# A two-layer diffusion trunk on one core: Silu of an expert's first tile ahead of a weight split, later waits for the last operand tiles, and filler products on TensorE

## What is computed

```python
def swiglu(h, w1, w3, w2):                       # layer 0: 1024 -> 2816 -> 1024
    return (jax.nn.silu(h @ w1) * (h @ w3)) @ w2

def moe_swiglu(h, router_w, router_b, w1, w3, w2):   # layer 1: 8 experts, 1024 -> 1024 -> 1024
    ...
    top_v, top_i = lax.top_k(logits, TOP_K)
    gates = jax.nn.softmax(top_v, axis=-1)
    ...
    hid = jax.nn.silu(jnp.einsum('nd,edf->enf', t, w1)) * jnp.einsum('nd,edf->enf', t, w3)
    hid = hid * dense_g.T.astype(hid.dtype)[:, :, None]
    return jnp.einsum('enf,efd->nd', hid, w2).reshape(b, s, d)
```

## Time and profile before

| | us |
|---|---|
| median of 3 runs | 1968.56 (1968.44 to 1970.23) |
| the profiled execution | 1969.62 |
| its span, first to last instruction | 1967.8 |
| PE busy | 1744.9 |
| DVE busy | 1162.0 |
| ACT busy | 649.0 |
| POOL busy | 259.3 |

### The profile page before, as it was taken

The page is one execution under the profiler, slowest core; times in us unless marked ns, Lnnn a source line. Parts: engine busy times, 40 slices in busy tenths (PEclk is TensorE's granted clock), DMA queues, the critical chain, the costliest instruction groups (busy, mean ns, idle before and its releaser), DMA issues.

```text
span 1967.8 us, 29448 instructions
## 1 busy us (share of the span) xinstructions
PE 1744.9 (89%) x11709; PEld 1589.2 (81%) x11709; DVE 1162.0 (59%) x1460; ACT 649.0 (33%) x769; POOL 259.3 (13%) x265
## 2 busy tenths in 40 slices
PE   0599689879999999997888989699999999999996
PEld 0599345779999999997864659588998998998996
DVE  7947567885465666658534663545555555655563
ACT  2221145233311211123322441543444344444431
POOL 3000102320000000003010123130110110110100
PEclk9999689889999999998995989889999999999998
DMA  8244000223344443433110001455555565565552
GB/s 345 70 155 143 20 0 1 86 86 129 101 137 147 149 150 128 160 128 98 65 44 3 0 0 65 179 180 177 203 184 175 200 198 168 208 193 174 208 187 60
DMA packets 45320, 251.13 MB, mean 128 GB/s; under 512 B 5516, under 2 KB 6172, under 8 KB 23888
## 3 DMA queue, kind: packets, MB, share of 16 engines
q1 hardware_dynamic: 28176, 192.17, 26.9%
q0 software_dynamic: 16512, 57.93, 10.1%
q10 hardware_dynamic: 576, 0.26, 0.0%
HBM read 236.68 MB, written 13.72 MB: 127 GB/s over the span
## 4 chain that ended last, share of the span: by engine, by line
PE 79%; DVE 9%; issue 6%; ACT 4%; DMA 1%; POOL 1%; ACTq 0%; DVEq 0%; SPq 0%; POOLq 0%
PE pp L610 55%; PE popr L610 5%; PE pm L610 5%; PE popr L773 4%; DVE popr L1225 3%; PE pp L876 2%; PE pp L727 1%; PE pm L708 1%; PE popr L713 1%; PE pm L753 1%; PE popr L770 1%; PE pm L756 1%; DVE tmpB L1252 1%; PE pm L700 1%; DVE h_lo L1270 1%
## 5 line engine op out<-in xcount | busy, mean ns | idle before, releaser
L1568 DVE TENSOR_TENSOR w_lo<-raw,w_hi 128x2048 fp32r<-128x2048 f32 x108 | 247.4, 2291 | 191.9 <-ACT w_hi L1136 191.9
L610 PE MATMUL pp<-g_hi,w_hi 128*128 128x192 f32 x1152 | 322.4, 280 | 21.3 <-ACT tmpA L1151 19.2
L610 PE MATMUL pp<-g_lo,w_hi 128*128 128x192 f32 x1152 | 321.4, 279 | 0.0
L610 PE MATMUL pp<-g_hi,w_lo 128*128 128x192 f32 x1152 | 321.3, 279 | 0.0
L610 PE MATMUL pp<-h_hi,w_hi 128*128 128x320 f32 x1152 | 267.2, 314 | 49.6 <-DVE h_lo L1270 44.8
L610 PE MATMUL pp<-h_lo,w_hi 128*128 128x320 f32 x1152 | 265.6, 312 | 0.0
L610 PE MATMUL pp<-h_hi,w_lo 128*128 128x320 f32 x1152 | 265.1, 312 | 0.0
L610 PEld LDWEIGHTS pp<-g_hi,w_hi 128*128 128x128 f32 x1152 | 227.4, 197 | 22.8 <-issue 22.8
L610 PEld LDWEIGHTS pp<-h_hi,w_hi 128*128 128x128 f32 x1152 | 195.3, 191 | 52.8 <-issue 51.6
L610 PEld LDWEIGHTS pp<-g_lo,w_hi 128*128 128x128 f32 x1152 | 227.6, 198 | 0.0
L610 PEld LDWEIGHTS pp<-g_hi,w_lo 128*128 128x128 f32 x1152 | 227.4, 197 | 0.0
(11 more groups left out here) (237 smaller groups left out, 3064.6 us busy)
## 6 DMA issues: line engine op xcount, KB each, us to landing
raw<-in_ws SPq DMA_DIRECT2D x164, 1024.0 KB, 4.8
modraw<-in_wmod POOLq DMA_DIRECT2D x80, 512.0 KB, 3.6
mod_first<-in_wmod SPq DMA_DIRECT2D x4, 2048.0 KB, 19.7
out_y<-six SPq DMA_DIRECT2D x7, 512.0 KB, 3.4
xT<-in_xT SPq DMA_DIRECT2D x1, 2560.0 KB, 20.3
token_rows<-tok SPq DMA_DIRECT2D x5, 512.0 KB, 2.6
mixer<-in_mixer SPq DMA_DIRECT2D x1, 1497.0 KB, 25.2
scond<-in_cond SPq DMA_DIRECT2D x1, 1024.0 KB, 5.1
```

The source lines that it names most:

```text
L610: ins = mm(out[:, at_bank(lo, hi)], x, y[:, lo:hi], start=f, stop=end)
L1568: V.tensor_tensor(w_lo[b][:], raw[b][:], w_hi[b][:].bitcast(F32), ALU.subtract).then_inc(w_lo_done, 1)
```

## The change

It has four parts. In each item, ACT now takes Silu of the first tile ahead of the split of slab 2, with no wait of its own for that split. PE starts the output part of an item when two `e_lo` tiles are still to come, and waits for these ahead of the matmuls that read them (`f` = 6 and 7). The same is done in the dense SwiGLU, by a new argument `late` of `slab`. And PE multiplies the two constants 40 times between `find_first` and the wait for the first item's rows, and 6 times behind each of its two gathers (`keep_pace`); nothing reads these products.

```diff
@@ slab
+            def slab(s, t, b_hi, b_lo, n=TOK, kk=KT, it=0, sstep=0, tstep=0, ready=None, order=range(KT), late=None):
...
                     for kt in range(kk):
+                        if late is not None and c == 0 and kt >= kk - 2:
+                            pe.wait_ge(prod_lo, late - kk + kt + 1)
@@ ffn
-                    pe.wait_ge(prod_lo, p)
+                    pe.wait_ge(prod_lo, p - 2)
                     with pe.Fori(0, 2) as i:
                         for c in range(2):
-                            slab(s + c, t + 2 * c, fh_hi, fh_lo, kk=hidden, it=i, sstep=2, tstep=4)
+                            slab(s + c, t + 2 * c, fh_hi, fh_lo, kk=hidden, it=i, sstep=2, tstep=4, late=None if c else p)
@@ experts, PE
+                def keep_pace(n):
+
+                    for _ in range(n):
+                        mm(prow[:, 0:P], ones, ident, start=True, stop=True)
...
                         if n == 0:
-                            pe.wait_ge(prod_lo, j * 8 + (P_MOE + 8))
+                            pe.wait_ge(prod_lo, j * 8 + (P_MOE + 6))
...
                             for f in range(8):
+                                if n == 0 and sl == 0 and f >= 6:
+                                    pe.wait_ge(prod_lo, j * 8 + (P_MOE + f + 1))
...
                 find_first()
+                keep_pace(40)
                 pe.wait_ge(rows_in, 32)
                 for x in range(2):
                     gather(0, x, T_MOE + x)
+                    keep_pace(6)
@@ experts, ACT
                     for i in range(4):
                         t = T_W13 + 4 * i
-                        act.wait_ge(tile_done, j * ITEM_TILES + (t if i else t + 1))
-                        hi_item(j, 2 * i + 2)
+                        if i:
+                            act.wait_ge(tile_done, j * ITEM_TILES + t)
+                            hi_item(j, 2 * i + 2)
                         for m in range(2):
                             act.wait_ge(tile_done, j * ITEM_TILES + (t + m + 1))
                             A(tA(m, CAP), pp[(t + m) % 2][:, 0:CAP], ACT.Silu).then_inc(tile_free[(t + m) % 2], 1)
+                            if i == 0 and m == 0:
+                                hi_item(j, 2)
```

More of the change, by code:

```diff
@@ L611, in three @@
                 return ins
-            def slab(s, t, b_hi, b_lo, n=TOK, kk=KT, it=0, sstep=0, tstep=0, ready=None, order=range(KT)):
+            def slab(s, t, b_hi, b_lo, n=TOK, kk=KT, it=0, sstep=0, tstep=0, ready=None, order=range(KT), late=None):
                 if ready is not None:
```

## The result

The changed kernel takes 1917.86 us (median of 4 runs, 1911.96 to 1919.77); the kernel before, run beside it, takes 1968.71 (4 runs, 1968.44 to 1970.23). The ratio is 0.9736, with a 95% interval from 0.9716 to 0.9756. The forecast was 1915.9. The profiled execution took 1919.68 with a span of 1917.9, so between the two profiled executions the span is 49.9 us shorter.

A forecast was written before the change was run, and what follows sets the result against it. PE, busy for 89% of the span, was taken as the bound, so gaps and low clock must go. 28.3 + 13.3 + 9.5 + 4.2 - 2.6 = 52.7 us off 1968.56 gave 1915.9 us; own range 1911 to 1920, with rival 1910 to 1924.

The forecast's parts named there:

- Part 1: Items 1 to 7: Silu of tile 0 ahead of slab 2's split ends PE's `tmpA` stall, gaining 28.3 us.
- 4.27: 384 matmuls of an item, 42.75 us against 47.02: 2.57 of stall, 1.63 of clock, 0.07 of rounding.
- three conditions: Items 1 to 7: one table load, ahead of the tile's wait; slab 2's later split harmless; queues behind cost PE nothing.
- second rival: ACT in items: table load stays behind the tile's wait, 4.3 us less gain, 1920.2 us; chance 0.09.
- Part 2: Late waits: `e_lo` gaps of nine items 13.3 us, three dense SwiGLU stalls 9.5 us, dense SwiGLU clock 4.2 us.
- first rival: The clock's falls are not owed to PE's stalls and stay: gain 38.7, 1929.9 us; chance 0.08.
- Part 3: `keep_pace` around item 0's gathers: buys nothing, as the DMA chain sets tile 4; a clock fall may lose 2.6 us.
- third rival: Slab weight loads become the bound, PE waits beyond 9.1 us per load; 1975 us at 9.72 us; chance 0.02.
- the fourth: Nothing changes, as slab loads at 9.65 us hold an item at its 75 us: 1968.6 us; chance 0.03.

The follow-up runs named there:

- the experiment with the second wait: Changed kernel with a second, long-met wait of ACT ahead of Silu of tile 0 in each item: 1923.06 us, ratio 0.9765.
- the last experiments: Changed kernel with SP loading slabs 3 and 4 of item 0 ahead of its slot-table wait: 1912.79 us with the constant products, 1912.76 without.
- the one with the filled stall: Kernel before, with 8 constant products put into the stall ahead of tile 2 of every item, Silu still late: 1963.84 us, ratio 0.9972.

## Why the prediction was right, step by step

**Part 1**, 28.3 us: right to the hundredth per item. 70.68 us from item to item with this part alone is 74.95 - 4.27, and item 8 was the right model for the changed item. Its three conditions held. The load went ahead of the wait (1351.90, tile at 1357.7), and the experiment with the second wait showed what it is worth, 4.6 us, beside the 4.3 that stood in the second rival. PE never waits for `tmpB` in items 1 to 7. And nothing queued behind `keep_to` or the slab loads made PE wait in items 1 to 7.

**Part 2**, 13.3 + 9.5 + 4.2: the gaps closed and no matmul waited. The dense SwiGLU gave 14.5 for 13.7, in which the stalls are 9.5 and the clock 5.0 where I had 4.2. The prediction added the items' 1.48 to the 4.27, and in the presence of part 1 that is right: 70.68 - 69.12 = 1.56 per item. As a price of the edit alone it is wrong, and so was my expectation of that experiment: alone it gives 5.5 us. The parts measured one by one give 25.8 + 5.5 + 12.9 - 0.5 = 43.7 us, the whole 50.9. The 7 us between them are, as far as the rows tell, the clock's: with the late waits alone the remaining stall takes 7.9 us more of lower clock, and with that stall filled or closed it takes none.

**The clock.** That the falls are owed to the stalls (the first rival denied it, at 1929.9 us) is shown by filling them: seven items of seven at 37.77 us. Why one item of the kernel before had the stall and no fall is not shown. The Trainium skill ("TensorE: Matmul & The Clock Gate", Why this matters for your kernels) allows a longer gap than these 2.4 us; the runs here don't agree with that allowance, as stalls of 2.40 us cost up to 3.25 us behind them, and closed or filled they cost none.

**Part 3**, nothing: shown twice, 1972.01 for 1971.51 alone and 1919.66 for 1917.86 when taken out. The reason given was SP's queue behind the table of slots, and the last experiments show it: with those two loads moved, the wait is gone. The idle time ahead of tile 4 was forecast at 7.5 us and was about 4.7. Tile 0 began 8.8 us behind the rows (1270.00 to 1278.76), not 7.0, as the clock was low in the first six products between the gathers; and slab 3's split came 19.6 us behind the rows, not 20.5. The rows themselves arrived 1.2 us later behind the routing than without the products, 16.4 us for 15.3 (from 1253.58 and 1263.49), which the prediction had at nothing: tile 0 takes some 2.5 us less and starts 2.2 us later. The price of a product, 0.24 us or more by rows of 32 columns, was near the 0.23 of 128 columns, with no reason given for the width not to count. The clock's loss behind the idle time was 2.1 us for a forecast of 2.6, and the e_lo gap of item 0 was gained.

**The term that was missing** is the 4.5 us of lower clock in the norm, the input projection and `qk_norm` of layer 1, whose code no edit touches. My own range had 2 us for clock falls in attention that shift by chance, but as a gain; as a loss it had only "here and there". Against it stand small errors the other way: 0.8 in the dense SwiGLU, 0.6 in item 0, 0.6 in items 1 to 8. By the two spans the gain is 52.7 + 0.8 + 0.6 + 0.6 - 4.5 - 0.3 = 49.9. The forecast of each edited stretch held within 0.8 us; that the total came within 2 us of the median, 1917.86, is in part luck, as 2.0 us of small errors stood against the missing 4.5.

The third rival (the weights) and the fourth (nothing) had no part in it: PE waits for no `w_lo` in the items at 69.12 us, nor in the version with item 0 shortened.

**Left open:** why the norm's clock falls in five executions and not in two of kernels that have the same code up to there, and why `qk_norm` is slow in just the seven executions whose program holds constant products further on. Open too is what makes the scatter between runs. The changed kernel had 8 us between its slowest and fastest run, where the kernel before had 2 in the same comparison, but in the three later ones, of more runs, the kernel before had 8 to 11, so nothing shows the scatter to be the change's.

## What to carry to other kernels

Where PE is the bound, price each of its gaps twice, by its length and by the clock behind it, and don't add up the worth of edits measured alone: while one gap stays, closing another can move the loss to it. When a small step on the path of the next tile stands behind a large one that only later work needs, turn them round, and see that a table load that the small step needs comes ahead of its wait. Before filling an idle stretch with dummy work, find out what the next piece of real work waits for; here it was a DMA queued behind an unrelated wait, and moving that DMA gained 6.9 us in the rows (3 to 5 in the medians), which the dummy work could not.

## What the hardware showed that was not expected

- A stall of 2.40 us, once per item, costs 0, 1.63 or 3.25 us of clock, in steps. In the kernel with items 1.48 us shorter the loss was one step larger in five of seven.
- A product of two 128x128 constants in plain float32 is two records of 0.115 us. Eight of them in a stall keep the clock at 1.00 behind it.
- A table load goes ahead of the wait of the ACTIVATE that needs it when one wait stands there, and behind the wait for the tile when a second one follows it. The Trainium skill ("ScalarE: Activation LUTs", Step-by-step) says only that the load is placed right before its ACTIVATE; the two kernels here differ by 0.66 us per item in just this.
- The 20 matmuls of layer 1's `qk_norm` took 5.56, 7.07 and 8.14 us in three kernels (before, changed, and the one with the filled stall) that have the same code there, at different granted clocks (1.00 and 0.78 in the first two).
- The DMA of the tokens to `token_rows` took 3.86 to 4.00 us in the five profiled executions with 40 products of PE at that place, and 2.88 to 2.94 in the four others whose chain holds it.
